# Sums of squares for a head-wise norm: one exact float32 multiplication by ones against two float32r ones on a split square

## The reference, cut to what matters

```python
def rms_norm(x, gain):
    xf = x.astype(jnp.float32)
    y = xf * lax.rsqrt(jnp.mean(xf * xf, axis=-1, keepdims=True) + EPS)
    return (y * gain.astype(jnp.float32)).astype(x.dtype)

def chunked_rel_attention(q, k, v, g_q, g_k, rel_bias):
    ...
    q = rms_norm(q, g_q)
    k = rms_norm(k, g_k)
    ...
```

## Time and profile before

| | us |
|---|---|
| median of 3 runs | 869.53 |
| lowest, highest | 867.52, 869.59 |
| the profiled execution's own time | 869.46 |
| its span in the trace | 867.8 |
| TensorE busy | 843.1 (97%) |
| VectorE busy | 522.5 (60%) |
| ScalarE busy | 388.7 (45%) |
| GpSimd busy | 138.3 (16%) |

### The profile page before, as it was taken

How to read it: one execution, slowest core, us unless ns; L and a number is a source line. 1 busy time by engine, 2 the same in 40 slices (tenths; PEclk the granted TensorE clock), 3 DMA queues, 4 the chain that set the end, 5 groups by cost and what they waited for, 6 DMA issues and landing times.

```text
span 867.8 us, 11900 instructions
## 1 busy us (share of the span) xinstructions
PE 843.1 (97%) x3953; PEld 693.1 (80%) x3953; DVE 522.5 (60%) x715; ACT 388.7 (45%) x557; POOL 138.3 (16%) x118
## 2 busy tenths in 40 slices
PE   5999999999999988999999999999999999999998
PEld 5788777787787777888888888888888888888886
DVE  5435768767467577455554666666666667533334
ACT  6435776655645535343435454333333334322221
POOL 2200222200100133000000312222222222200000
PEclk9999999999999999999999999999999999999999
DMA  6333223221312322333334332333333333222223
GB/s 199 99 97 98 68 78 98 75 71 49 97 48 69 89 72 86 99 93 99 97 95 135 97 97 78 96 96 96 96 96 96 97 96 96 98 97 96 97 97 121
DMA packets 126634, 81.50 MB, mean 94 GB/s; under 512 B 5028, under 2 KB 116360, under 8 KB 126608
## 3 DMA queue, kind: packets, MB, share of 16 engines
q1 hardware_dynamic: 125936, 79.04, 30.1%
q0 software_dynamic: 672, 2.12, 1.0%
HBM read 79.03 MB, written 2.12 MB: 94 GB/s over the span
## 4 chain that ended last, share of the span: by engine, by line
PE 83%; DVE 9%; ACT 3%; issue 2%; POOL 1%; DMA 1%; SPq 1%; ACTq 0%; DVEq 0%; POOLq 0%
PE ps L1182 25%; PE ps L1184 25%; PE ps L1183 25%; DVE suffix L909 2%; PE ps L1257 1%; PE ps L1269 1%; DVE pt_lo L932 1%; PE ps L1283 1%; PE ps L1284 1%; DMA w_raw<-in_w_in_dram 1%; DVE pa L916 1%; PE ps L1236 1%; DVE w_lo L799 1%; DVE out_sb L1172 1%; POOL o_lo L381 1%
## 5 line engine op out<-in xcount | busy, mean ns | idle before, releaser
L799 DVE TENSOR_TENSOR w_lo<-w_raw,w_hi 128x1024 fp32r<-128x1024 f32 x141 | 175.4, 1244 | 182.0 <-ACT w_hi L463 142.7
L1182 PE MATMUL ps<-h_lo,w_hi 128*128 128x512 f32 x704 | 277.4, 394 | 1.4 <-ACT gates L576 0.6
L1184 PE MATMUL ps<-h_hi,w_lo 128*128 128x512 f32 x704 | 274.2, 389 | 0.0
L1183 PE MATMUL ps<-h_hi,w_hi 128*128 128x512 f32 x704 | 274.1, 389 | 0.0
L463 ACT ACTIVATE w_hi<-w_raw 128x1024 fp32r<-128x1024 f32 x126 | 133.6, 1060 | 313.3 <-PE ps L1184 313.2
L1182 PEld LDWEIGHTS ps<-h_lo,w_hi 128*128 128x128 f32 x704 | 132.2, 188 | 28.9 <-issue 2.2
L1184 PEld LDWEIGHTS ps<-h_hi,w_lo 128*128 128x128 f32 x704 | 132.2, 188 | 28.0
L1183 PEld LDWEIGHTS ps<-h_hi,w_hi 128*128 128x128 f32 x704 | 132.3, 188 | 26.5 <-issue 0.2
L1182 PE MATMUL ps<-w_lo,a_hi 128*128 128x512 f32 x176 | 68.5, 389 | 0.0
L1183 PE MATMUL ps<-w_hi,a_hi 128*128 128x512 f32 x176 | 68.5, 389 | 0.0
L1184 PE MATMUL ps<-w_hi,a_lo 128*128 128x512 f32 x176 | 68.5, 389 | 0.0
(11 more groups left out here) (186 smaller groups left out, 1125.3 us busy)
## 6 DMA issues: line engine op xcount, KB each, us to landing
w_raw<-in_w_in_dram SPq DMA_DIRECT2D x104, 256.0 KB, 3.1
w_raw<-in_w_up_dram SPq DMA_DIRECT2D x88, 256.0 KB, 3.1
w_raw<-in_w_down_dram SPq DMA_DIRECT2D x44, 256.0 KB, 2.8
w_raw<-in_w_out_dram SPq DMA_DIRECT2D x16, 256.0 KB, 3.0
x_in<-in_x_dram SPq DMA_DIRECT2D x4, 512.0 KB, 6.3
bias_rev<-rel_bias_rows POOLq DMA_DIRECT2D x8, 256.0 KB, 3.5
x_re<-in_x_dram SPq DMA_DIRECT2D x2, 1024.0 KB, 6.0
w_raw<-in_w_branch_a_dram SPq DMA_DIRECT2D x8, 256.0 KB, 2.7
```

Of the source, the lines that this page charges most:

```text
L799: v.tensor_tensor(w_lo[:, slot, :], w_raw[:, slot, :], r32(w_hi[:, slot, :]), ALU.subtract)\
L1182: mm3(dst, l_hi, r_lo, start=start, stop=False, **kw)
L1183: mm3(dst, l_hi, r_hi, start=False, stop=False, **kw)
L1184: return mm3(dst, l_lo, r_hi, start=False, stop=stop, **kw)
```

## The change

The squares are written by ScalarE twice: as float32 in `sq` and as float32r in `qk_hi` (the high part). VectorE subtracts them into `qk_lo` (`squares_lo`, new), behind the softmax scaling of head 1 for the query, and behind `lo(b + 2)` for the key; in the prologue both stand behind `lo(N_VA + 1)`. `sumsq` becomes two float32r multiplications by `ones_heads_r`, low part first, and waits for the low part. The raw copy comes after the two squares. The key's `sumsq` moves from ahead of `transposes(s, 1)` to behind it. TensorE waits for the raw copies ahead of the two gate tiles, which overwrite their banks. Cut are only the declarations of the semaphore and of the float32r ones.

```diff
@@ scalar @@
                 if prev:
                     a.wait_ge(qk_lo_ready, t - 1)
+                act(qk_hi[:, i, :], ps[:, bank, :], ACT.Square)
+                act(sq[:, i, :], ps[:, bank, :], ACT.Square).then_inc(proj_sq, 1)
                 act(qk_raw[:, i, :], ps[:, bank, :], ACT.Copy).then_inc(proj_raw, 1)
-                act(sq[:, i, :], ps[:, bank, :], ACT.Square).then_inc(proj_sq, 1)
@@ vector @@
             v.memset(ones_heads[HD:P, HD:P], 1.0).then_inc(heads_step, 1)
+            d.wait_ge(heads_step, 2)
+            v.tensor_copy(ones_heads_r[:, :], ones_heads[:, :]).then_inc(heads_step, 1)
...
+            def squares_lo(t, i):
+
+                d.wait_ge(proj_sq, t + 1)
+                v.tensor_tensor(qk_lo[:, i, :], sq[:, i, :], r32(qk_hi[:, i, :]), ALU.subtract).then_inc(sq_lo_ready, 1)
...
             lo(N_VA + 1, 1)
+            squares_lo(0, 0)
+            squares_lo(1, 1)
             lo(N_VA + 2, 0)
...
                 if proj == "B":
                     raw_lo(t, 0)
+                if proj == "A":
+                    squares_lo(t, 0)
                 lo(b + 2, 0)
                 if proj == "B":
                     raw_lo(t + 1, 1)
                 if proj == "A":
+                    squares_lo(t + 1, 1)
                     newton_half_q(s + 1)
                 pt_split_lo(s, 1)
@@ tensor @@
             def sumsq(t, i, bank):
 
-                pe.wait_ge(proj_sq, t + 1)
-                mm3(ps[:, bank, :], ones_heads[:, :], sq[:, i, :], start=True, stop=True).then_inc(ss_done, 1)
+                pe.wait_ge(sq_lo_ready, t + 1)
+                mm3(ps[:, bank, :], ones_heads_r[:, :], qk_lo[:, i, :], start=True, stop=False)
+                mm3(ps[:, bank, :], ones_heads_r[:, :], qk_hi[:, i, :], start=False, stop=True).then_inc(ss_done, 1)
...
                 output(s, 0)
                 if proj == "A":
                     sumsq(t, 0, HEAD[0] + 1)
+                transposes(s, 1)
+                if proj == "A":
                     sumsq(t + 1, 1, HEAD[0] + 2)
-                transposes(s, 1)
+                    pe.wait_ge(proj_raw, t + 1)
                 if proj == "B":
                     pe.wait_ge(qk_lo_ready, s * 2 + 3)
                 elif proj == "U":
                     pe.wait_ge(u_stored, 1)
                 tile_of(b + 2, 0, PROJ[0])
                 output(s, 1)
+                if proj == "A":
+                    pe.wait_ge(proj_raw, t + 2)
```

More of the change, by code:

```diff
@@ L96, in build @@
         ones_all = sb("ones_all", [P, P])
+        ones_heads_r = sb("ones_heads_r", [P, P], F32R)
         g_row = sb("g_row", [KD, P])
@@ L178, in build @@
         v_stored, v_b_stored = sem("v_stored"), sem("v_b_stored")
-        proj_raw, proj_sq = sem("proj_raw"), sem("proj_sq")
+        proj_raw, proj_sq, sq_lo_ready = sem("proj_raw"), sem("proj_sq"), sem("sq_lo_ready")
         ss_done, ms_done, lnq_done, expq_done, newton_step, rn_ready = (
```

## The result

| | kernel before | changed kernel |
|---|---|---|
| median, us | 869.48 (21 runs, 867.50 to 870.16) | 870.65 (21 runs, 868.66 to 872.32) |
| ratio | | 1.0016, 95% interval 1.0010 to 1.0023 |
| the profiled execution's own time, us | 869.46 | 871.27 |
| its span, us | 867.8 | 869.6 |
| scores of slot 0 start, us | 73.11 | 71.68 |

The account below looks back on a forecast made before the run. From the key's sum on, a slot was taken to be bound by the chain on the other engines, not TensorE's passes. 869.46 - 0.80 (prologue) + 3 x 0.90 (slots) = 871.36, plus 0.07 for the median: 871.4 us; range 869.2 to 873.6.

Parts of the forecast that it names:

- this chain: Slots 0 to 2: key's sum through ScalarE, VectorE, POOL and o_sum to the next scores, 13.90 us without a gap.
- Rival (1): Slots 0 to 2: TensorE's passes count, each slot gives 0.86 us, total 866.2 us; chance 0.08.
- rival (2): Slots: VectorE isn't late for the key's sum, only TensorE's order counts; 3 x 0.72 - 0.80, 870.9 us; chance 0.14.
- A query's pass: Slots: the query's first pass waits for VectorE's subtraction, starting at 88.91 instead of 88.52, 0.39 us late.
- The key's sum: Slots 0 to 2: behind the transposes and VectorE's queue, it reaches ScalarE 0.90 us later per slot, +2.70 in all.
- The prologue: Pair 0's sums: four float32r passes take 0.92 us instead of 1.72, a gain of 0.80 reaching slot 0's scores.
- The waits: Each of slots 0 to 2: scores wait about 1.0 us for o_sum, the second output some 0.5 for pt_lo.
- Slot 0: Scores to scores, slot 0 takes 32.2 us instead of 31.3.
- TensorE was taken to wake 0.14 us after VectorE's end: Slots: TensorE starts about 0.14 us after the VectorE instruction it waits for, read from o_sum and scores.
- The wait on VectorE for the key: Slots: VectorE's key low part lets TensorE start at 90.65, later than TensorE's own 90.47 by 0.18 us.
- Rival (3): Slots: subtractions collide with POOL, over 0.8 us each; at 1.43 each 875.9 us; chance 0.12 in whole or part.

Follow-up runs that it names:

- the move alone: Kernel before, float32 arithmetic kept, with only the key's sum put behind the second transposes: ratio 1.0035 against the kernel before.
- key's sum ahead again: Changed kernel with the key's sum ahead of the second transposes again, VectorE's order untouched: ratio 1.0019 against the kernel before.
- two spare passes: Kernel before with two spare float32r multiplications of 128x512 on TensorE behind the key's sum in each of slots 0 to 2: ratio 0.9996.
- prologue alone: Kernel before with the change made in the prologue only, slots 0 to 2 keeping the old sums: ratio 0.9986.
- slots alone: Kernel before with the change made in slots 0 to 2 only, the prologue keeping the old float32 sums: ratio 1.0033.
- repetition: The changed kernel, unedited, run and profiled again beside the kernel before: ratio 1.0015.
- the last experiment: Changed kernel, both subtractions before low weights, key's sum before transposes, high passes first, query's Ln and Exp before key's Ln: 866.09 us, 0.9966 against kernel before.

## Why the prediction was right

**The direction and the mechanism.** "From the key's sum on, a slot is as long as this chain" held in every run that tested it: the move alone (no pass saved, +3.0 us), key's sum ahead again (1 us of waiting added on TensorE, nothing lost), two spare passes (nothing), prologue alone (the gain lands). Rival (1), that the passes count, expected the opposite sign for slots alone and 0 for the move; both are out. The time of the whole alone would not have decided between the forecast and rival (2): that put 870.9, +1.4 us, which is nearer to what was measured than the forecast's 871.4. What decides are the slots, 2.69, 2.54 and 2.47 us longer in the profiles of the changed kernel, of its repetition and of slots alone, where rival (2) wanted 3 x 0.72 = 2.16, and the run with the key's sum ahead again.

**The terms.** A query's pass was forecast 0.39 us late by VectorE: in the changed kernel it starts at 87.50, where the passes of output(s, 0) ahead of it end, start to next start, at 87.11 (the view lists 0.23 of this as the wait; about 0.3 was forecast). The key's sum was forecast 0.90 us late in each slot; measured from scores to scores the slots grew by 0.94, 0.86 and 0.89, in sum 2.69 for 2.70. The prologue was forecast at -0.80: 0.91 in the chain for 1.72 is -0.81. That it reaches 73 us shows the time from the first projection tile to the scores of slot 0: 56.72 to 56.77 us in the five kernels whose prologue has the old sums, 55.85 to 56.07 in the seven profiles with the new ones. The waits were forecast at about 1.0 and 0.5 and are 0.97 and 0.44 to 0.5. Slot 0 was forecast at 32.2 us and is 32.22. That the slots' sum fits to 0.01 us is partly luck. TensorE was taken to wake 0.14 us after VectorE's end, and it is 0.05 to 0.06; in slots 0 and 2 VectorE comes to the subtractions 0.11 us later after the scores than to the weights before, as one softmax scaling lasts 0.11 to 0.13 longer.

**The wait on VectorE for the key.** Forecast 0.18 us late. Here TensorE's transposes end (start to next start) at 88.07 + 1.01 = 89.08, VectorE at 88.50 + 0.68 = 89.18, and the pass starts at 89.24: 0.16. The view of waits doesn't list it: its three entries for L1250 are the query's. But in all three slots the key's pass starts 0.06 us after VectorE's end, as the query's pass does behind its listed wait. So by these rows rival (2), VectorE not late, is out, though by 0.16 us a slot only.

**POOL.** Rival (3) wanted subtractions of over 0.8 us. All eight last the same in the first profile:

```profile
L841 DVE TENSOR_TENSOR qk_lo<-sq,qk_hi x8: 683/684/685, 30.8 to 154.6; 128x512 fp32r<-128x512 f32 x8
```

In the repetition seven do and one, in the prologue, takes 0.84, where 0.8 was the mark; TensorE doesn't wait for it. The collisions that the earlier trace rows suggested exist, but elsewhere, and one run turned one off. The Newton product of 1.43 us, beside POOL's, takes 0.69 all four times in the last experiment:

```profile
L847 DVE TENSOR_TENSOR nt<-nt,sq x4: 691/692/693, 36.8 to 154.2; 128x512 f32<-128x512 f32 x4
```

There it starts 0.51 us ahead of POOL's product (91.10 and 91.61 in slot 0), in the kernel before 0.16 behind it (93.50 and 93.34). The Trainium skill ("SBUF — State Buffer", section "SBUF: two separate sides") states the lock that would explain both; the runs show only that the same instruction has two lengths, the long one where it starts behind POOL's and the short one where it starts ahead.

**What was off.** The whole came out 0.3 to 0.5 us under the forecast: +1.4 by the ratio for +1.9. The intervals of both measurements hold +1.9. The first profile's 1.81 is made of other parts than forecast. The prologue came out 1.43 us early, of which 0.56 stand already at the first projection tile (15.83 instead of 16.39 us), ahead of anything the change touches; across the kernels of this study slot 0's scores start between 71.60 and 73.39. And behind slot 7 the changed kernel's profile is 0.6 us longer, beside a lower clock of TensorE (below). These two nearly cancel. Counted from the first projection tile, the prologue gains 0.87 us in both profiles of the changed kernel, and with the slots (2.69 and 2.54) that makes +1.8 and +1.7. Grouping the executions by their mean clock, as in the table below, gives +1.6. What keeps the ratio another 0.2 lower I can't name.

## What to carry to other kernels

The busiest engine's share says little about a stretch that ends with a wait on another engine: follow the chain from that wait back to the instruction where it leaves the busy engine, and ask of every edit when *that* instruction ends, not how much work it saves. A cheaper operation that needs a new partner operand is only as early as the partner's place in its engine's queue; put the partner first, and let the part that needs no partner go ahead. Test slack by adding work to it: two spare passes cost one run and say more than a sum. And count as slack every wait behind the added work that doesn't depend on it, not only the next one.

## What the runs showed of the hardware

In slot 7 TensorE waits 3.5 us for pt_lo, and in most executions it then works for a while at the lower of its clock's two levels. The first multiplication behind that wait, in the kernel before and in the changed one:

```profile
312.27 0.64 PE L1283 MATMUL ps<-pt_lo,v_st 128*128 128x512 f32 x1 [3.47 <-DVE pt_lo L932]
312.71 0.63 PE L1284 MATMUL ps<-pt_hi,v_st 128*128 128x512 f32 x1
```

```profile
313.49 0.77 PE L1298 MATMUL ps<-pt_lo,v_st 128*128 128x512 f32 x1 [3.48 <-DVE pt_lo L943]
314.05 0.63 PE L1299 MATMUL ps<-pt_hi,v_st 128*128 128x512 f32 x1
```

A pass of 128x512 starts 0.44 and 0.56 us before the next where 0.23 is usual. Windows of 4 us there (time, busy time of the engines, then granted clock, DMA share and GB/s), of before and after:

```profile
312.00:316.00 4.00, 3.73 (x16) 3.57 (x17) 1.25 (x2) 0.00 (x0) 0.00 (x0) 0.57 0.36 104
316.00:320.00 4.00, 4.00 (x21) 3.33 (x20) 2.27 (x2) 3.30 (x4) 0.00 (x0) 1.00 0.09 27
```

```profile
312.00:316.00 4.00, 2.51 (x9) 2.35 (x10) 2.48 (x2) 0.00 (x0) 0.00 (x0) 0.50 0.08 20
316.00:320.00 4.00, 4.00 (x18) 3.62 (x18) 0.47 (x1) 1.74 (x2) 0.00 (x0) 0.64 0.38 111
```

The clock is back at full at 316 us in one, and still at 0.64 on average in the next window of the other, though both waited the same. In the profile of the last experiment, with the same wait of 3.5 us, it doesn't fall at all; in the other eleven it is below full only between 300 and 330 us. The mean clock varies between executions of one kernel. The executions of both kernels that stand beside a clock in this study, grouped by it:

| mean granted clock | before, median us (runs) | changed, median us (runs) | difference |
|---|---|---|---|
| 1.0 | 867.36 (7) | 869.00 (7) | +1.64 |
| 0.997 to 0.998 | 868.93 (32) | 870.57 (16) | +1.64 |
| up to 0.996 | 870.13 (29) | 871.69 (10) | +1.56 |

The medians of the groups lie 2.7 to 2.8 us apart, about twice what the change costs and most of what lies between the fastest and the slowest run in the table of the result (2.7 and 3.7 us). That it is this one stretch in the executions without a profile too is inferred from the twelve that have one. With an effect of this size, a comparison of few runs can be decided by it.
